# Adding the last pair of expert blocks by one-hot products, the other rows by accumulating DMAs, over a zeroed row memory

## The reference, cut to what matters

```python
def hier_moe(h, rg_w, rg_b, re_w, re_b, w_gate, w_up, w_down):
    ...
    for g in range(N_GROUPS):
        hid = jax.nn.silu(jnp.einsum('td,edf->tef', t, w_gate[g])) * jnp.einsum('td,edf->tef', t, w_up[g])
        y = y + jnp.einsum('tef,efd->td', hid * combine[:, g, :, None], w_down[g])
    return y.reshape(B, L, D)

def trunk_layer(x, c, gla_s0, k_cache, v_cache, slopes, p):
    ...
    x = layer_norm(DEEPNORM_ALPHA * x + gt1 * mix, ln1_g, ln1_b)
    h2 = x * (1 + sc2) + sh2
    x = layer_norm(DEEPNORM_ALPHA * x + gt2 * hier_moe(h2, rg_w, rg_b, re_w, re_b, w_gate, w_up, w_down), ln2_g, ln2_b)
    return x, s_new.astype(x.dtype), k_new, v_new
```

## Time and profile before

| | |
|---|---|
| three runs | 716.08, 720.27, 723.23 us; median 720.27 |
| the profiled execution | 721.39 us, of which the trace's span is 719.6 |
| mean granted TensorE clock | 0.920 of full speed |
| busy, share of the span | PE 83%, DVE 47%, ACT 19%, POOL 14% |
| DMA | 180.98 MB, mean 252 GB/s |

### The profile page before, as it was taken

How to read it: one execution, slowest core, us unless ns; L and a number is a source line. 1 busy time by engine, 2 the same in 40 slices (tenths; PEclk the granted TensorE clock), 3 DMA queues, 4 the chain that set the end, 5 groups by cost and what they waited for, 6 DMA issues and landing times.

```text
span 719.6 us, 10926 instructions
## 1 busy us (share of the span) xinstructions
PE 595.0 (83%) x4530; PEld 373.0 (52%) x4530; DVE 335.8 (47%) x600; ACT 135.2 (19%) x356; POOL 103.2 (14%) x144
## 2 busy tenths in 40 slices
PE   3679999899987687999836999887788887769884
PEld 2559999676764364444525655443344444335330
DVE  2463441555542662595685344433333333343348
ACT  1441450244332153011111100000000000000100
POOL 3000000100001013000021233222222222212100
PEclk9969999999998599999955999999998999999996
DMA  8991321002006989810399799999999999996162
GB/s 299 370 247 60 68 63 56 16 1 102 16 1 237 364 319 261 301 56 32 134 409 369 290 414 412 411 410 408 411 412 410 410 409 409 407 405 271 48 248 96
DMA packets 71289, 180.98 MB, mean 252 GB/s; under 512 B 22165, under 2 KB 26109, under 8 KB 66629
## 3 DMA queue, kind: packets, MB, share of 16 engines
q1 hardware_dynamic: 60612, 163.39, 60.9%
q0 software_dynamic: 7936, 14.09, 5.6%
q10 hardware_dynamic: 2688, 2.77, 1.1%
HBM read 176.25 MB, written 14.45 MB: 265 GB/s over the span
## 4 chain that ended last, share of the span: by engine, by line
PE 46%; SPq 27%; DMA 10%; DVE 10%; ACT 4%; issue 3%; DVEq 0%; POOLq 0%; ACTq 0%
SPq L431 27%; PE bank L947 8%; PE bank L1193 8%; PE bank L1014 6%; PE bank L1297 5%; DMA ring<-in_moe_w_up_dram 3%; DMA ring<-in_ada_w_dram 3%; PE bank L1371 3%; PE bank L901 2%; PE bank L1315 2%; PE bank L996 2%; DMA x_tok<-in_x_sample_dram 2%; PE bank L1038 1%; PE bank L1055 1%; PE bank L1283 1%
## 5 line engine op out<-in xcount | busy, mean ns | idle before, releaser
L1297 PE MATMUL bank<-late_w,xT 128*64 128x256 f32 x672 | 83.4, 401 | 20.9 <-DMA late_w<-in_moe_w_up_dram 18.0
L1799 DVE COPY xT<-bank 128x512 f32<-128x512 f32 x38 | 26.2, 692 | 125.0 <-PE bank L1283 124.4
L1297 PE MATMUL bank<-ring,xT 128*64 128x256 f32 x480 | 64.7, 426 | 20.4 <-DMA ring<-in_moe_w_up_dram 18.6
L1297 PEld LDWEIGHTS bank<-late_w,xT 128*64 128x64 f32 x672 | 49.6, 139 | 60.9 <-DMA late_w<-in_moe_w_up_dram 28.6
L1297 PEld LDWEIGHTS bank<-ring,xT 128*64 128x64 f32 x480 | 36.9, 148 | 52.2 <-DMA ring<-in_moe_w_up_dram 27.6
L843 ACT ACTIVATE sgl<-bank 128x128 f32<-128x128 f32 x36 | 10.0, 277 | 246.9 <-PE bank L1297 246.8
L602 POOL DMA_INDIRECT expert_rows<-ye,dsti x36 | 36.5, 1014 | 125.7 <-DVE ye L1818 125.7
L595 POOL DMA_INDIRECT xg<-h_scratch,srci x38 | 39.2, 1031 | 102.5 <-PE bank L1283 89.0
L1815 DVE SCALAR_TENSOR_TENSOR S<-bank,modrt,S 128x512 f32<-128x512 f32 x36 | 27.0, 750 | 32.6 <-PE bank L1315 32.3
L1315 PE MATMUL bank<-late_w,hT 128*64 128x512 f32 x168 | 40.7, 605 | 0.0
L1014 PE MATMUL bank<-ring_r,h_high 128*128 128x512 f32 (+1 forms) x140 | 38.2, 413 | 0.0
(11 more groups left out here) (315 smaller groups left out, 860.2 us busy)
## 6 DMA issues: line engine op xcount, KB each, us to landing
ring<-in_ada_w_dram SPq DMA_DIRECT2D x22, 1024.0 KB, 11.1
late_w<-in_moe_w_gate_dram SPq DMA_DIRECT2D x21, 1024.0 KB, 16.8
late_w<-in_moe_w_up_dram SPq DMA_DIRECT2D x21, 1024.0 KB, 22.4
late_w<-in_moe_w_down_dram SPq DMA_DIRECT2D x21, 1024.0 KB, 22.4
ring<-in_moe_w_down_dram SPq DMA_DIRECT2D x15, 1024.0 KB, 22.7
ring<-in_moe_w_gate_dram SPq DMA_DIRECT2D x15, 1024.0 KB, 16.5
ring<-in_moe_w_up_dram SPq DMA_DIRECT2D x15, 1024.0 KB, 22.6
ring<-in_w_in_dram SPq DMA_DIRECT2D x7, 1024.0 KB, 5.6
```

The lines of the kernel that those rows point to most:

```text
L1297: mm = pe.matmul(bank[2 + a][f * C:(f + 1) * C, 0:2 * P], x, w[:, kk, f, :, :], start=(kk == 0), stop=(kk == KD - 1))
```

## The change

Four things change; the numbers are those of two taken overflow pairs.

Row memory. Right after its constants POOL writes zeros over the used part of `yb_d` by four DMAs (L541 to L545 of the changed kernel), 4.46 MB from a zeroed 1 KB piece of `S` in each partition, and waits for them (`s_zero`) ahead of its third gather.

Scatters. POOL holds back each pair's scatters until the next pair, and waits for the landing of a pair's scatters (`scattered`) before it goes on. The last pair is never scattered. After the last branch POOL adds the rows in DRAM onto the scaled x by five DMAs with `accum_op=ALU.add` (`ROW_SUMS`): sample first rows, prompt first rows (four tiles, 2.10 MB), sample second rows, then the second rows of tiles 0 and 1 and of tiles 2 and 3 (1.05 MB each), each second one after the landing of its first.

Products. POOL makes a table of half-row numbers; for the two blocks of a pair DVE compares it with the blocks' row numbers (`hot_rows`) into two one-hot matrices `late_hot` of 128 x 544. This is done ahead of the first overflow pair and again in each pair. PE adds x by the identity as before, and then the last pair by `late_hot` times `ye` straight from SBUF: four products of 64 rows for each tile. The sample's tile goes first (`FINAL`).

Norm. DVE takes the statistics and multiplies by g, ACT makes the square root, the negative mean times it, and scales and shifts PSUM into x, POOL adds b, except for the last tile, where DVE does.

```diff
+            zeros = S[:, 0, :, :].rearrange("p a v -> p (a v)").unsqueeze(1)
+            for k in range(2):
+                top = yb_d[k * 2 * KSTEP:k * 2 * KSTEP + 2 * LP, :].rearrange("(p a) (b n) -> p (a b) n", p=P, b=2)
+                end = yb_d[k * 2 * KSTEP + 2 * LP:k * 2 * KSTEP + 2 * T, :].rearrange("p (b n) -> p b n", b=2)
+                pool.dma_start(top, zeros.broadcast_to([P, 4 * LP // P, 2 * DV])).then_inc(s_zero, 16)
+                pool.dma_start(end, zeros[0:2 * LS].broadcast_to([2 * LS, 2, 2 * DV])).then_inc(s_zero, 16)
             pool.wait_ge(tok_ev, NT)
...
+            pool.wait_ge(x_al, NT)
+            firsts = {}
+            for i, (js, k) in enumerate(ROW_SUMS):
+                if k == 1:
+                    pool.wait_ge(s_sum[firsts[js[0]]], 16)
...
+                    pool.dma_start(x_tok[:, js[0]:js[-1] + 1, :], rows[P * js[0]:P * (js[-1] + 1), :].rearrange("(j p) n -> p j n", p=P),
+                                   accum_op=ALU.add).then_inc(s_sum[i], 16)
...
+                act.wait_ge(r_chain, q + 1)
+                for half in range(2):
+                    act.activation(x_tok[0:r, j, half * 512:(half + 1) * 512], bank[SUM_BANKS[q][half]][0:r, :], ACT.Identity,
+                                   scale=st[:, 13:14], bias=st[:, 14:15]).then_inc(f_z, 1)
...
+            for q in range(3):
+                sum_x(q)
+            pe.wait_ge(late_rows, 1)
+            for q in range(3):
+                sum_late(q)
...
+            def hot_rows(b):
+                dve.tensor_scalar(late_hot[b % 2], half_rows, row_of[:, b:b + 1], None, ALU.is_equal)
...
-                for half in range(2):
-                    c = slice(half * 512, (half + 1) * 512)
-                    link(dve.scalar_tensor_tensor(x[:, c], bank[SUM_BANKS[j][half]][0:ROWS[j], :], st[:, 12:13], ln2[0:ROWS[j], 0, c],
-                                                  ALU.subtract, ALU.mult))
-                dve.wait_ge(f_l, j + 1)
-                dve.scalar_tensor_tensor(x, x, st[:, 13:14], ln2[0:ROWS[j], 1, :], ALU.mult, ALU.add).then_inc(f_o, 1)
+                dve.wait_ge(f_z, 2 * (q + 1))
+                dve.tensor_tensor(x, x, ln2[0:ROWS[j], 0, :], ALU.mult).then_inc(f_g, 1)
+                if q == NT - 1:
+                    dve.wait_ge(f_g, NT)
+                    dve.tensor_tensor(x, x, ln2[0:ROWS[j], 1, :], ALU.add).then_inc(f_last, 1)
```

More of the change, by code:

```diff
@@ L467, in _ @@
                         load(e, k, 2)
[L470 to L477, removed]
+            for q, j in enumerate(FINAL):
+                sp.wait_ge(*((f_o, q + 1) if q < NT - 1 else (f_last, 1)))
                 dst = y_prompt[0, P * j:P * (j + 1), :] if j < NP else y_sample[0]
@@ L605, in scatter, with scattered @@
                     bounds_check=4 * KSTEP - 1, oob_is_err=False).then_inc(s_sc[a], 16)
+            def scattered(n):
+                for a in range(2):
+                    pool.wait_ge(s_sc[a], 16 * n)
             gather(0, 0)
@@ L620, in _ @@
                     for b in (E + 2 * i, E + 2 * i + 1):
+                        scatter(b - 2, b % 2)
+                    for b in (E + 2 * i, E + 2 * i + 1):
                         if b + 2 < NBLK:
@@ L1347, in _, with sum_x, sum_late @@
                     pe.wait_ge(xe_ev, min(E + 2 * i + 4, NBLK))
-            def sum_out(j):
-                return [bank[i][0:ROWS[j], :] for i in SUM_BANKS[j]]
-            def sum_x(j):
+            def sum_x(q):
+                j = FINAL[q]
                 r = ROWS[j]
[L1355 to L1371, removed]
-                mm.then_inc(pe_sum, 1)
+                pe.wait_ge(s_sum[[i for i, (js, k) in enumerate(ROW_SUMS) if j in js][-1]], 16)
+                for half in range(2):
+                    pe.matmul(bank[SUM_BANKS[q][half]][0:r, :], ident[0:r, 0:r], x_tok[0:r, j, half * 512:(half + 1) * 512],
+                              start=True, stop=False)
+            def sum_late(q):
+                j = FINAL[q]
+                for a in range(2):
+                    for half in range(2):
+                        hs = slice(half * C, (half + 1) * C)
+                        mm = pe.matmul(bank[SUM_BANKS[q][half]][0:ROWS[j], :], late_hot[a][hs, tok(j)], ye[hs, a, :],
+                                       start=False, stop=(a == 1))
+                mm.then_inc(pe_sum, 1)
+            for q in range(3):
[3 more added lines that the diff above has]
+                sum_late(q)
+            for q in range(3, NT):
+                if q == 4:
+                    pe.wait_ge(f_z, 2)
+                sum_x(q)
+                sum_late(q)
         @block.vector
@@ L1881 @@
+            for q in range(NT + 1):
+                if q < NT:
+                    spread(q)
+                if q >= 1:
+                    times_g(q - 1)
 _INS = ["x_prompt", "x_sample", "c_prompt", "c_sample", "state_gla", "cache_swa_k", "cache_swa_v",
```

76 lines of the change are left out of this document (51 added, 25 removed).

## The result

The changed kernel takes **738.55 us** in the median of four runs (735.36 to 741.85), the kernel before 718.17 us beside it: a ratio of **1.026**, with an interval of 1.022 to 1.031. It is slower, by 19 us. The prediction had 727.2 us and a range that ended at 738.0: the sign was right, the size was a third of what came. The profiled execution took 740.64 us with a span of 738.9 us; before, 721.39 and 719.6.

What follows compares the result with a forecast made beforehand. DMA engines were taken to bound the start, weights the experts' stage, then a 54.9 us tail. Start +9.8 and tail -2.9 gave +6.9 us on the median 720.27: 727.2 us, range 712 to 738.

Steps and rivals of the forecast that it cites:

- the sum of the tail: Adds, late products, norm and last store after the experts: end at 716.7 us against 719.6, 2.9 us gained.
- The start: Zeroing DMAs beside SP's full queue take 0.28 of 375 GB/s and delay the last `ada_w` unit by 9.8 us.
- upper bound: Start: all 4.46 MB of zeros at 375 GB/s come out of the last `ada_w` unit's time, 11.9 us.
- The rival in which the zeros lose against SP's queue: Start: zeros drain in the pause after 53 us, costing 1.4 us or nothing; 718.8 us, chance 0.25.
- The adds onto x: Tail: adding DMAs make three passes, 273 GB/s, plus 2.6 us fixed; landings at 680.9 and 687.4 us.
- should reads alone count, 205: Tail: adds at 205 GB/s, landings at 683.6 and 691.4 us, tail 1.0 us later than now.
- the rival with dear adds: Tail: adds slower than 273 GB/s; 731.1 us at 205 GB/s, 739 at 137; chance 0.25.
- The products: PE behind the adds: eight rows of x take 5.5 us, the first late tile 1.94, done at 694.9 us.
- the late `ye`: Last expert rows, ready at 679.1 us instead of 677.0, hidden behind the adds.
- The norm: DVE's norm of five tiles, split with ACT and POOL, takes 19.4 us instead of 25.9.
- this price, 1.8 us: Norm: by the skill's page the last product waits for POOL's addition, 1.8 us more; left out of the sum.
- The end: Behind DVE's last instruction: 2.4 us to store the last tile, ending at 716.7 us before the start's delay.

Runs made afterwards that it cites:

- e1: The changed kernel with its four zeroing transfers issued behind the cache stores, at about 142 us planned, instead of at 9.7 us: 728.69 us, ratio 1.0125.
- e2: The kernel before with only the four zeroing transfers at the start and the wait for them added: 729.0 us, ratio 1.0152.
- e3: The changed kernel with the five transfers onto x overwriting x instead of adding to it: 733.01 us, ratio 1.0180.
- e5: The changed kernel with b added to the last two tiles on VectorE, so GpSimd adds it to three tiles, not four: 736.18 us, ratio 1.0245.
- e7: The kernel before with only the norm split as in the changed kernel: 725.44 us, ratio 1.0063.
- e4: The kernel before with a one-element memset on GpSimd behind the last output tile: 723.44 us, ratio 1.0074.
- e6: The changed kernel with zeros behind the cache stores, rows loaded plainly and added by GpSimd and VectorE, GpSimd adding b to two tiles: 715.45 us, ratio 0.9952.
- e8: e6 with VectorE's two one-hot tables made at the start of each pair, before GpSimd's additions: 716.33 us, ratio 0.9954 to the kernel before.
- e10: e8 with the sample tile's two rows and one of the third tile's added by PE matmuls, the third's other by VectorE: 723.66 us, ratio 1.0040.

## Why the prediction came out as it did

What failed is the sum of the tail. It priced the adds at 273 GB/s where they moved at 210, took the last product without a neighbour, and had no term for GpSimd's drain behind its last addition.

**The start: right in size (+9.8 us; measured +10.0, e1 -9.8, e2 +10.9).** The step's working was not. It took pieces of 1 KB and a small share beside SP's queue. The trace has 4 KB pieces, and all of the 4.46 MB went ahead of the last unit, which is the case that the prediction kept as its upper bound (11.9 us at 375 GB/s); its working has 0.105 MB per us and so 3.7 MB. What brought the cost down to 10.0 us is that the engines were busier: between 9.7 us and the landing of the last unit they moved 13.90 MB at 386 GB/s, before 9.58 MB at 368. Too few bytes and too low a rate cancelled, so the 9.8 is luck. The rival in which the zeros lose against SP's queue fell.

**The adds onto x: mis-sized, and the first cause of the miss.** The prompt's add was issued at 679.6 us, where the prediction with its start has 679.9. The step "an add reads the row and x and writes x, three passes instead of two, 273 GB/s" failed. The DMA engines were full at about 210 GB/s, half of the 410 of plain loads (e3): the case "should reads alone count, 205". The page "Collectives: The Full Stack" of the Trainium skill, section "Why ReduceScatter is half of AllGather", has the two reads as its reason and 1.93 as its ratio; the runs here have 410 / 210 = 1.95 and so agree, on an add within one core; no run here shows the reason itself. Also the fixed part of 2.6 us, taken from a scatter, was too small: 15.37 us less 2.23 MB at 210 GB/s leaves 4.8, and 8.32 us less 1.05 MB leaves 3.3. Together the two landings took 23.7 us instead of 17.2, which is 6.5 us. Of the rival with dear adds the mechanism was therefore right, and its 731.1 lacked the end.

**The products: right.** Eight rows of x took 5.45 us (5.5 taken), the first late tile 1.86 (1.94 taken; one after the other eight rows take 3.43): products in the two halves of the rows do run beside each other. DVE, and not PE, set the pace behind them, and the late `ye` (689.8) stayed hidden behind the adds, as the prediction had it.

**The norm: 19.4 us predicted, 20.8 measured.** The difference is the last product, 2.77 us instead of 1.26, beside POOL's addition. The prediction had this price, 1.8 us, in the sentence on the Trainium skill's page "SBUF — State Buffer", section "Who interferes with whom", and left it out of the sum. The trace agrees with that page: 1.22 us where no addition runs (e5), 2.55 (e7) and 2.77 where one does.

**The end: the step that was missing.** The sum kept the 2.4 us that stood behind DVE's last instruction. Measured were 7.1. The prediction asked what POOL's additions of b hide behind, and not what follows on POOL when they are done: the drain of 9 us, which the trace of before shows at 677.9 us, off every path. Moving POOL's last work from 677.8 to 729.5 us put it on the path (e4, e7).

In the frame of the profiled executions, the prediction's end was 716.7 + 9.8 = 726.5 us, and the span was 738.9. The 12.4 us between them are 6.5 for the adds, 1.4 for the product and 4.7 behind it (12.6; the adds were issued 0.3 early). The tail that was to gain 2.9 us lost 9.3.

That the start is worth 10 us is shown by two runs from both sides; the rate of the adds by one; the drain by e4 and e7. The value of the shorter end in the changed kernel is shown in traces alone.

## What to carry to other kernels

Ask of each engine not only what its new work lies beside, but what follows when it is the last: an end-of-program drain that nobody waits for becomes the end of the kernel once that engine works to the end. Here an adding DMA took as long for its bytes as a plain one for twice as many (210 and 410 GB/s), so price it at half the plain rate before letting it replace loads and additions that an idle engine could make. And put clearing of memory where the DMA engines are empty, even if the source is ready sooner: the same four transfers cost 10 us when issued at 10 us, and at 135 us nothing that the runs show.

## What the runs showed of the hardware that was not expected

- GpSimd's drain at the end of the program ends 8.7 to 9.2 us after the end of its last instruction in all twelve traces, behind a scatter (8.9 in the kernel before), a memset of one element (9.0) and additions (9.2 in the changed kernel). ACT's and DVE's end with their last instruction.
- GpSimd and VectorE slow each other by more than one instruction. In e6 a table of VectorE, one SBUF tensor and a column, went from 0.49 to 4.87 us, two whole additions of GpSimd, and additions on both sides at once took up to 3.3 us instead of 2.34 (GpSimd) and 1.22 (VectorE). For the tables the Trainium skill's page "SBUF — State Buffer", section "Who interferes with whom", says that a tensor-scalar operation too can take the port pair shared with GpSimd, and that whoever comes second is shut out for a whole instruction; the trace agrees for the first table (2.40 us, one addition), and the second was shut out for two additions in a row. What reads PSUM was not slowed (0.74 us beside the additions and without them).
- After the last expert block PE stands for 5.1 us in e6, e8 and e10 and for 2.8 in the kernel before, put down to "issue". It is no wait for GpSimd's additions (e10). Nothing run here tells what it is; in the kernels with transfers to wait for it is hidden.
